# A two-block transformer: token order of five RWKV sources by full-array transpositions, and three small reductions in full-array records

## The reference

```python
def wkv_scan(s0, decay, k, v, kk, a, r, reverse):
    def step(S, inp):
        w_t, k_t, v_t, kk_t, kka_t = inp[:5]
        S = (S * w_t[:, :, None, :]
             - jnp.einsum('bhij,bhj->bhi', S, kk_t)[..., None] * kka_t[:, :, None, :]
             + v_t[..., None] * k_t[:, :, None, :])
        y = jnp.einsum('bhij,bhj->bhi', S, inp[5]) if emit else None
        return S, y
...
kk = kk * lax.rsqrt(jnp.maximum(jnp.sum(kk * kk, axis=-1, keepdims=True), 1e-24))
...
var = jnp.mean(jnp.square(y - mean), axis=-1, keepdims=True)
yn = ((y - mean) * lax.rsqrt(var + GN_EPS)).reshape(B, L, D_MODEL) * ln_g + ln_b
```

## Time and profile before

| | |
|---|---|
| median of the runs | 3081.94 us |
| the profiled execution, its own time | 3091.67 us |
| its span in the trace | 3089.9 us |
| mean granted TensorE clock | 0.947 |
| the eight rounds (start of the first to the end of the eighth) | 1252.5 to 1869.3 us |

### The profile page before, as it was taken

One profiled execution on the slowest core, in us unless ns is written; L12 is line 12 of the kernel. 1 busy time (PEld: TensorE's weight loads), 2 busy tenths in 40 slices (PEclk: granted clock), 3 DMA queues, 4 the chain that ended last, 5 costly groups with the idle time before them and its releaser, 6 DMA issues. The chain is left out here.

```text
span 3089.9 us, 72809 instructions
## 1 busy us (share of the span) xinstructions
PE 2705.3 (88%) x32492; PEld 2378.1 (77%) x32492; DVE 1848.7 (60%) x2902; ACT 1134.9 (37%) x1786; POOL 31.7 (1%) x46
## 2 busy tenths in 40 slices
PE   4988989999997998677777777899998898889998
PEld 4977989999996887566666676688886685678887
DVE  7656775655546643766666665755567644466642
ACT  4326343222224432533444333433334415454421
POOL 0011000000000000000000000000000000000000
PEclk9999989999996999799999998899998998999999
DMA  6320224444321333000000003355531210123332
GB/s 257 117 88 27 89 85 130 126 130 140 120 75 55 113 103 128 24 22 25 25 25 25 25 10 116 126 179 176 179 111 57 68 36 8 55 77 101 96 94 84
DMA packets 89958, 272.52 MB, mean 88 GB/s; under 512 B 9440, under 2 KB 14688, under 8 KB 89568
## 3 DMA queue, kind: packets, MB, share of 16 engines
q1 hardware_dynamic: 85088, 258.17, 25.5%
q10 hardware_dynamic: 4608, 10.49, 1.0%
HBM read 252.11 MB, written 16.52 MB: 87 GB/s over the span
## 5 line engine op out<-in xcount | busy, mean ns | idle before, releaser
L427 DVE TENSOR_TENSOR weights_low<-raw_weights,weights_high 128x1024 fp32r<-128x1024 f32 (+3 forms) x333 | 356.4, 1072 | 703.4 <-ACT weights_high L396 702.6
L396 ACT ACTIVATE weights_high<-raw_weights 128x1024 fp32r<-128x1024 f32 (+3 forms) x333 | 310.9, 935 | 970.9 <-PE psum L223 928.9
L223 PE MATMUL psum<-mlp_in_high,weights_high 128*128 128x512 f32 (+1 forms) x1120 | 370.3, 367 | 21.5 <-DVE mlp_in_low L964 16.4
L223 PE MATMUL psum<-mlp_in_low,weights_high 128*128 128x512 f32 (+1 forms) x1120 | 369.0, 366 | 0.0
L223 PE MATMUL psum<-mlp_in_high,weights_low 128*128 128x512 f32 (+1 forms) x1120 | 368.7, 366 | 0.0
L223 PEld LDWEIGHTS psum<-mlp_in_high,weights_high 128*128 128x128 f32 x1120 | 208.1, 189 | 49.3 <-issue 17.6
L223 PE MATMUL psum<-hidden_high,weights_high 128*128 128x384 f32 (+1 forms) x768 | 229.5, 352 | 0.0
L223 PE MATMUL psum<-hidden_low,weights_high 128*128 128x384 f32 (+1 forms) x768 | 229.5, 352 | 0.0
L223 PE MATMUL psum<-hidden_high,weights_low 128*128 128x384 f32 (+1 forms) x768 | 229.4, 352 | 0.0
L223 PEld LDWEIGHTS psum<-mlp_in_low,weights_high 128*128 128x128 f32 x1120 | 208.4, 189 | 23.9
L223 PEld LDWEIGHTS psum<-mlp_in_high,weights_low 128*128 128x128 f32 x1120 | 208.1, 189 | 24.0
(11 more groups left out here) (470 smaller groups left out, 5248.7 us busy)
## 6 DMA issues: line engine op xcount, KB each, us to landing
raw_weights<-in_mlp_w SPq DMA_DIRECT2D x96, 512.0 KB, 4.3
mod_space<-in_ada SPq DMA_DIRECT2D x56, 512.0 KB, 3.6
pool_u<-in_ada SPq DMA_DIRECT2D x56, 512.0 KB, 3.6
raw_weights<-in_w_up SPq DMA_DIRECT2D x44, 512.0 KB, 3.6
work<-in_ada SPq DMA_DIRECT2D x32, 512.0 KB, 4.9
raw_weights<-in_mlp_w SPq DMA_DIRECT2D x64, 256.0 KB, 3.1
raw_weights<-in_w_down SPq DMA_DIRECT2D x16, 512.0 KB, 3.5
raw_weights<-in_w_in SPq DMA_DIRECT2D x12, 512.0 KB, 4.7
```

The source lines that it names most:

```text
L223: last = nc.tensor.matmul(out[:, a, :] if wide else out, w[:, cols], x[:, at, t0:t1], start=first, stop=final)
L396: nc.scalar.activation(halves_of(ph, j)[0], raw_of(ph, j), ACT.Copy).then_inc(high.sem, 1)
L427: nc.vector.tensor_tensor(lo, raw_of(ph, j), hi.bitcast(F32), ALU.subtract).then_inc(split.sem, 1)
```

## The change

Five of the seven sources (V, both A, both KD) are turned by six 128 x 128 transpositions each; EXC stays at 24 small matmuls. V with A of direction 0, and A of direction 1 with KD of direction 0, share a batch of twelve over banks 4 to 6, with one count for TensorE and two keeps on ACT; so five batches take the place of seven, and each stands at another job of the list. `bonus` goes to bank 6, `step` and `ystate` to bank 7. `sums` and `yvar` are six and four matmuls of 128 x 128 weights on two columns. `root` and `groot` write their root widened over the head, 768 and 512 columns from a repeated input, and `spread` and `yspread` transpose that, six and four times; DVE's products with them are one instruction each. `bonus`, `sums`, `small` and `root` stand one job earlier. The waits of K, E, P and B for their turned sources name the same sources as before; E, which needs both EXC, now waits for the last batch of all. In the diff empty and unchanged lines are left out, and with them those four waits and the new bank numbers of `step`, `ystate`, `ysum` and of the bonus on DVE.

```diff
@@ -2077,10 +2077,10 @@
     at = {("M", 0): [("tok", 0), ("step", 1)], ("N", 0): [("tok", 1), ("step", 2)],
-          ("I", 0): [("tok", 2), ("step", 3)], ("M", 1): [("tok", 3), ("step", 4)],
-          ("N", 1): [("tok", 4), ("step", 5)], ("I", 1): [("square", 0), ("tok", 5), ("step", 6)],
-          ("M", 2): [("tok", 6), ("bonus", 0), ("step", 7)], ("N", 2): [("sums", 0), ("step", 8)],
-          ("I", 2): [("small", 0), ("root", 0), ("lora", 0), ("step", 9)], ("K", 0): [("lora", 1), ("step", 10)],
+          ("I", 0): [("step", 3)], ("M", 1): [("tok", 2), ("step", 4)],
+          ("N", 1): [("tok", 3), ("step", 5)], ("I", 1): [("square", 0), ("tok", 4), ("bonus", 0), ("step", 6)],
+          ("M", 2): [("sums", 0), ("step", 7)], ("N", 2): [("small", 0), ("root", 0), ("step", 8)],
+          ("I", 2): [("lora", 0), ("step", 9)], ("K", 0): [("lora", 1), ("step", 10)],
@@ -2193,7 +2193,9 @@
-    TURN, BONUS, PREPS = 6, 13, 14
+    TURN, BONUS, PREPS = 6, 11, 12
+    TURNS = ("V", "A0"), ("A1", "KD0"), ("KD1",), ("EXC0",), ("EXC1",)
+    TURNED = sum(TURNS, ())
@@ -2263,6 +2265,7 @@
+        ROOTS = sb("wkv_roots", [P, SEQ])
@@ -2569,31 +2572,43 @@
                     if name == "tok":
-                        src = (V[:, :], EXC[:, 0, :], EXC[:, 1, :], A[:, 0, :], A[:, 1, :], KD[:, 0, :], KD[:, 1, :])[n]
-                        if n == 0:
-                            pe.wait_ge(v_loaded.sem, v_loaded.base + 16 * (k + 1))
-                        if k or n >= 5:
-                            pe.wait_ge(tilded.sem, tilded.base + k + 1)
-                        elif n >= 1:
-                            pe.wait_ge(first_tilded.sem, first_tilded.base + 2)
-                        pe.wait_ge(*(turn_kept(k, n - 1) if n else prep_kept(k, 2)))
-                        if n == 0 and k >= 2:
-                            pe.wait_ge(pair_done.sem, pair_done.base + k - 1)
-                        for p in range(tiles):
...
-                            t = tile_of((n - 1) % 2, p) if 1 <= n <= 4 else p
-                            for o in range(2):
-                                for h in range(2):
-                                    f, to = rows_of(h), rows_of(p % 2 if 1 <= n <= 2 else o)
-                                    c = (p // 2 * 2 + o if 1 <= n <= 2 else p) * CHUNK
-                                    last = nc.tensor.matmul(ps[to, 4 + h, c:c + CHUNK], src[f, at_chunk(t, o)], EYE[f, :],
-                                                            start=True, stop=True)
+                        for m, what in enumerate(TURNS[n]):
+                            at = TURNED.index(what)
+                            source = {"V": V[:, :], "EXC0": EXC[:, 0, :], "EXC1": EXC[:, 1, :], "A0": A[:, 0, :], "A1": A[:, 1, :],
+                                      "KD0": KD[:, 0, :], "KD1": KD[:, 1, :]}[what]
+                            if what == "V":
+                                pe.wait_ge(v_loaded.sem, v_loaded.base + 16 * (k + 1))
+                                pe.wait_ge(*prep_kept(k, 2))
+                                if k:
+                                    pe.wait_ge(*by_vector(k - 1, "F", GROUPS - 1))
+                                if k >= 2:
+                                    pe.wait_ge(pair_done.sem, pair_done.base + k - 1)
+                            elif m == 0:
+                                pe.wait_ge(*turn_kept(k, at - 1))
+                            if k or what in ("KD0", "KD1"):
+                                pe.wait_ge(tilded.sem, tilded.base + k + 1)
+                            elif what != "V":
+                                pe.wait_ge(first_tilded.sem, first_tilded.base + 2)
+                            for p in range(tiles):
+                                if what in ("EXC0", "EXC1"):
+                                    t = tile_of(int(what[3]), p)
+                                    for o in range(2):
+                                        for h in range(2):
+                                            f, c = rows_of(h), (p // 2 * 2 + o) * CHUNK
+                                            last = nc.tensor.matmul(ps[rows_of(p % 2), 4 + h, c:c + CHUNK], source[f, at_chunk(t, o)],
+                                                                    EYE[f, :], start=True, stop=True)
+                                else:
...
+                                    t, to = (tile_of(int(what[1]), p), p % 2 * 3 + p // 2) if what in ("A0", "A1") else (p, p)
+                                    lo = 4 * 512 + m * T0 + to * P
+                                    last = nc.tensor.transpose(flat[:, lo:lo + P], source[:, t * P:(t + 1) * P], core.ident[:, :])
...
                     elif name == "bonus":
...
+                        pe.wait_ge(*turn_kept(k, TURNED.index("KD0")))
                         for h in range(2):
...
-                            last = nc.tensor.matmul(ps[f, 7, :], core.ones[f, 0:HEAD], BON[f, :], start=True, stop=True)
+                            last = nc.tensor.matmul(ps[f, 6, :], core.ones[f, 0:HEAD], BON[f, :], start=True, stop=True)
@@ -2611,11 +2626,8 @@
                         pe.wait_ge(squared.sem, squared.base + q + 1)
...
-                            for o in range(2):
-                                for h in range(2):
-                                    f = rows_of(h)
-                                    last = nc.tensor.matmul(ps[rows_of(o), 4 + h, t:t + 1], SQ[f, at_chunk(t, o)], core.ones[f, 0:1],
-                                                            start=True, stop=True)
+                            last = nc.tensor.matmul(ps[:, 4, 2 * t:2 * t + 2], SQ[:, t * P:(t + 1) * P], core.head_sum[:, 0:P:HEAD],
+                                                    start=True, stop=True)
@@ -2623,12 +2635,9 @@
                         pe.wait_ge(rooted.sem, rooted.base + q + 1)
...
-                            for h in range(2):
-                                for o in range(2):
-                                    f, c = rows_of(o), h * tiles + t
-                                    last = nc.tensor.matmul(ps[rows_of(h), 4 + o, t * CHUNK:(t + 1) * CHUNK],
-                                                            small[f, 0, 1, c:c + 1].to_broadcast([HEAD, HEAD]), EYE[f, :],
-                                                            start=True, stop=True)
+                            last = nc.tensor.transpose(flat[:, 4 * 512 + t * P:4 * 512 + (t + 1) * P],
+                                                       KK[:, t * P:(t + 1) * P],
+                                                       core.ident[:, :])
@@ -2670,21 +2679,15 @@
                     elif name == "yvar":
...
-                            for o in range(2):
-                                for h in range(2):
-                                    f = rows_of(h)
-                                    last = nc.tensor.matmul(ps[rows_of(o), 4 + h, tiles + t:tiles + t + 1], CSQ[f, at_chunk(t, o)],
-                                                            core.head_mean[f, h * HEAD:h * HEAD + 1], start=True, stop=True)
+                            last = nc.tensor.matmul(ps[:, 5, 2 * t:2 * t + 2], CSQ[:, t * P:(t + 1) * P], core.head_mean[:, 0:P:HEAD],
+                                                    start=True, stop=True)
...
                     elif name == "yspread":
...
-                            for h in range(2):
-                                for o in range(2):
-                                    f, c = rows_of(o), h * xt + t
-                                    last = nc.tensor.matmul(ps[rows_of(h), 4 + o, t * CHUNK:(t + 1) * CHUNK],
-                                                            small[f, 1, 1, c:c + 1].to_broadcast([HEAD, HEAD]), EYE[f, :],
-                                                            start=True, stop=True)
+                            last = nc.tensor.transpose(ps[:, 4, t * P:(t + 1) * P],
+                                                       ROOTS[:, t * P:(t + 1) * P],
+                                                       core.ident[:, :])
@@ -2727,21 +2730,19 @@
                     if name == "tok":
                         eng.wait_ge(prep_done.sem, prep_job(k, TURN + n))
-                        src = ps[:, 4:6, 0:tiles * CHUNK].rearrange("p h (t c) -> p h t c", c=CHUNK)
-                        if 1 <= n <= 2:
-                            d = n - 1
-                            dst = RHS[:, :, :, 2 * d:2 * d + 2, 0, :].rearrange("p i o h c -> p h (i o) c")
-                        elif 3 <= n <= 4:
-                            d = n - 3
-                            dst = AG[:, 2 * d:2 * d + 2, :, :, 0, :].rearrange("p j i h c -> p h i j c")
-                            for h in range(2):
-                                last = act(dst[:, h, :, :, :], src[:, h, :, :].rearrange("p (i j) c -> p i j c", j=2), ACT.Copy)
-                            last.then_inc(prep_s.sem, 1)
-                            return
```

(35 more changed lines are left out.)

18 lines of the change are left out of this document (9 added, 9 removed).

## The result

| | median us | runs | ratio to the kernel before, 95% |
|---|---|---|---|
| before | 3082.47 | 3079.83 to 3084.26 | |
| changed | 3055.71 | 3052.46 to 3061.24 | 0.9913 (0.99 to 0.9925) |
| changed, a second time, beside another set of runs of before (3083.09) | 3054.65 | 3049.45 to 3061.62 | 0.9908 (0.9892 to 0.9923) |

The change saves 27 to 28 us. The forecast was 3047, a saving of 35; the result lies inside the range and 8 to 9 us above the forecast. The profiled execution of the changed kernel took 3061.24 us, 30.4 less than that of before.

What follows compares the result with a forecast made beforehand. It took the first part of a round to be bound by TensorE's instruction fetch; 21.6 + 2.5 + 3.3 + 7.2 = 34.6 us, rounded to 35, taken from the median gave 3047 us, range 3020 to 3072.

Steps and rivals of the forecast that it cites:

- What bounds it: First part of a round: bound by the number of TensorE's instructions, fed at some 3.7 us for 256.
- By fetch alone 13.4 us: Up to the end of N of group 2: 454 records, 3.57 packets of 3.75 us, 13.4 for 19.2 us.
- rival (a): Fetch is all: every saved packet counts, 7.7 us a round, 60 in all, 3022 us; chance 0.15.
- By waits alone: First part with fetch free: ACT round trips set it; `sums` at 12.6 us, TensorE through N of group 2 at 14.4.
- the stall: First part: of 3.6 remaining fetch stalls of about 1 us, one, 1.0 us, lands on the chain.
- Switching shapes: 14 changes a round between four 64 x 64 arrays and one full array: 0.1 us each, 1.4 us a round.
- Rival (c): Each change of array shape drains TensorE, 0.45 us on the chain: 15 us slower, 3097 us; chance 0.05.
- The last part: Last part of a round: 52 records fewer, at most 1.6 us, against a longer `groot`; 0.9 us taken.
- the cover of `groot`: Last part: 1.1 us between the root's end and TensorE's `yspread`, gone if TensorE comes a whole microsecond earlier.
- The sum: Rounds 1 to 6 21.6 us, round 0 2.5, round 7 3.3, last part 7.2: 34.6 us saved, rounded to 35.
- (b): Round's first part: stalls hide behind waits for two keeps; gain 1.3 us a round, 10 in all, 3072 us; chance 0.18.
- (d): ACT's repeated input or keep across two banks runs at half speed, about 4 us a round lost, 3080 us; chance 0.07.

Runs made afterwards that it cites:

- e1_turn_only: Kernel before with V, both A and both KD turned by six 128x128 transpositions each, in seven single batches at the old places: 3061.19 us, ratio 0.9929.
- e11_two_turned: Kernel before with KD of both directions alone turned by six 128x128 transpositions: 3074.27 us, ratio 0.997.
- the four kernels above: Before (3082.47 us); before with two KD sources transposed (3074.27); before with five sources transposed in seven batches (3061.19); the changed kernel (3055.71).

## Why the prediction came out as it did

*What bounds it.* Right in kind: the "issue" gaps inside runs of like matmuls are TensorE without instructions; they fell from 28 to 2 in six rounds as records were taken out, and the half of the change that cuts the sources' records gives 22 of 28 us. What it expected to be left was too much: 3.6 stalls of about 1 us in the first part, where the first profile shows one stall up to N of group 2 in each of two rounds and none in four. The Trainium skill, "Runtime: NRT & Kernel Launch", Instruction fetch mechanics, calls such crossings "mostly hidden": up to N of group 2 they are so in the changed kernel, with 0.2 us a round of such stalls, and are not in the kernel before, with 3.7.

*"By fetch alone 13.4 us"* and rival (a), which rests on it, were impossible, and the trace of before said so: TensorE is busy for 15.0 us in that stretch, so no removal of instructions could end it sooner, and the text itself had found that TensorE's own time hardly changes. *"By waits alone"*, 14.4 us to the same place, fails by the same check: 15.0 us of work and 0.7 for `sums` do not fit into it. The check "652/127 = 5.13 packets, 3.75 us each" was circular: it divides the length by the count, and would have come out whatever bound the stretch. The right reading of the same row is 19.22 - 15.02 = 4.2 us of idle, the ceiling of the term; measured per round, 4.4 idle went to 1.3.

*"By waits alone"*, the term on which the sum stood. The steps of round 3 on TensorE:

```profile
1473.84 0.87 PE L2604 MATMUL psum<-constants,wkv_v 128*128 128x128 f32 x6
1474.55 0.82 PE L2604 MATMUL psum<-constants,wkv_a 128*128 128x128 f32 x6
...
1476.97 0.87 PE L2604 MATMUL psum<-constants,wkv_a 128*128 128x128 f32 x6 [0.76 <-ACT wkv_a_ga L2745]
...
1480.71 0.87 PE L2604 MATMUL psum<-constants,wkv_kd 128*128 128x128 f32 x6
...
1484.51 0.92 PE L2598 MATMUL psum<-wkv_eye,wkv_exc_rho 64*64 64x64 f32 x46 [0.21 <-ACT residual L2745]
...
1487.38 1.50 PE L2629 MATMUL psum<-constants,wkv_kk 128*128 128x2 f32 x12
...
1492.53 0.88 PE L2622 MATMUL psum<-lora_input,wkv_ups 64*64 64x384 f32 x8 [1.70 <-DVE wkv_small L2908]
```

and on ACT:

```profile
1475.40 0.81 ACT L2745 ACTIVATE work<-psum 128x768 f32<-128x768 f32 x1 [11.67 <-PE psum L2604]
1476.11 0.81 ACT L2745 ACTIVATE wkv_a_ga<-psum 128x768 f32<-128x768 f32 x1
...
1492.68 0.84 ACT L2762 ACTIVATE wkv_kk<-wkv_small 128x768 f32<-128x768 f32 x1 [6.33 <-DVE wkv_small L2910]
1493.54 1.28 ACT L2754 ACT_TABLE_LOAD   x1
1494.83 1.05 ACT L2754 ACTIVATE wkv_decay<-psum,wkv_parameters 128x384 f32<-128x384 f32 x2
```

| from the round's start, us | forecast | measured |
|---|---|---|
| second batch begins | 3.7 | 3.8 |
| `sums` begins | 12.6 | 14.2 |
| `sums` takes | 0.7 | 1.5 |
| TensorE through N of group 2 | 14.4 | 16.9 |
| `small` ends on DVE | 17.8 | 19.4 |
| ACT's first `lora` keep | 20.0, with the stall 21.0 | 21.6 |
| loop begins | 29.6 | 30.0 |

The batches, the keeps (0.81 us, also across the banks) and the root (0.84 us for the 0.81 taken) came as worked out. Two terms were too small. What comes on top of the batches (11.9 us) was given 0.7 us; it took 2.3, most of it since TensorE works in order: KD1's transpositions stand behind M of group 1 and come 0.7 us after their bank is free, EXC0 0.2 us late behind N of group 1, and `sums` behind the bonus and M of group 2, 1.0 us after ACT's last keep. And `sums` was priced as six transpositions, 0.66 us, although the prediction itself counts 12 records for it; it took 1.50. What made up for it: in this round no stall of fetch landed on the chain, where 1.0 us had been put, DVE's `small` came 2.5 us after TensorE where 3.4 had been allowed, and the chain from `lora` to the loop gave 0.5 us where 0.3 was forecast (8.88 to 8.34 us from ACT's first `lora` keep). So the first part lost 3.4 us in the mean of six rounds for the 3.6 forecast (3.5 in the second profile): a right total in which a stall that did not come paid for work that had been left out. That the total came out is luck.

*Switching shapes.* Right: 0.1 us each. The transpositions begin 0.06 us before the last 64 x 64 record of M ends (1473.21 + 0.69 against 1473.84), where like follows like at 0.17. Rival (c) is out by this and by the result; the drain of which "TensorEngine Tiling (Array Packing)" of the Trainium skill, Key Properties, speaks has this price here.

*The last part.* Forecast 0.9 us, measured 0.8 and 1.0. The terms are not those of the forecast: the cover of `groot` is gone, as it had warned (TensorE waits 0.36 us in round 3), and `yvar` takes 1.05 us in 8 records where 32 took 0.64; the shorter stalls pay for both.

*The sum.* Rounds 1 to 6 gave 4.2 and 4.5 us each in the two profiles, for 4.5. Round 0 gave 3.6 and 0.5 for 3.4, round 7 5.5 and 3.3 for 4.2. The sum for the rounds, 34.6, stands against 34 and 31. The medians show 27 to 28. The difference lies outside the rounds or in the profiled executions themselves: that of before was 9.7 us above its median, the two of the changed kernel 5.5 and 4.1; a round's saving read off a slow execution of before was taken in full from the median. Part of it can be placed: round 0 starts at 1252.5 us in that execution and between 1246.6 and 1249.2 in all eleven other profiles, at 1246.8 and 1246.6 in the two (`e1_turn_only`, `e11_two_turned`) whose code up to there is that of before. So some 6 of its 9.7 us lie ahead of the rounds, and no more than 4 can be in the 34 and 31 read off it. How the rest divides was not settled.

*The rivals.* (a) out, as shown. (b) lives in part: waits for ACT did come into the open, at 1 us a round and not the 3.5 that it takes back, and what took the place of fetch up to N of group 2 is above all TensorE's own work in order, busy for 94% of it. (d) is out: keep and root run at the speed forecast.

## What to carry to other kernels

Cutting the instructions of an engine that starves for them, while its work stays the same, gives back its idle time in that stretch and no more; read length less busy time first, and hold every forecast of the stretch, by fetch or by waits, against the busy time. Then ask which chain is late next: here starting `small`, `root` and the chain behind them one job earlier, with no work saved, gave 24 us, nearly as much as the whole change. And a fuller array isn't a cheaper record: price each shape by its own count of records.

## What the runs showed of the hardware that was not expected

- A matmul of 128 x 128 f32 weights on only two columns costs two transpositions. `sums` in the changed kernel, and the weight load of a transposition (`yspread`), each min/median/max ns:

```profile
L2629 PEld LDWEIGHTS psum<-constants,wkv_kk x12: 186/192/192, 1487.4 to 1488.6; 128*128 128x128 f32 x12
L2629 PE MATMUL psum<-constants,wkv_kk x12: 251/251/272, 1487.4 to 1488.6; 128*128 128x2 f32 x12
```

```profile
L2688 PEld LDWEIGHTS psum<-constants,wkv_roots x32: 137/142/231, 1390.6 to 1848.8; 128*128 128x128 f32 x32
```

  The weight load of a record is listed at 192 ns and that of a transposition at 142, but the records follow one another just as closely: (1.50 - 0.25)/11 = 0.11 us for `sums`, (0.87 - 0.27)/5 = 0.12 us for six transpositions of a source. The difference is the count: six matmuls leave twelve records, six transpositions six. The 48 small records that `sums` had before take 0.96 us, 0.02 each, so undoing it made the first part 0.4 us a round shorter with four times the records.
- Stalls on instructions vanish faster than the packets. The stretch up to N of group 2 is about 5.3, 4.6, 3.6 and 3.6 packets of 127 matmul records in the four kernels above, and the stalls are 3.7, 2.7, 0.6 and 0.2 us a round. TensorE's own work for a packet is 2.9, 3.3, 4.2 and 4.4 us (busy time by packets), and a packet took 3.50 to 3.70 us where it starved: stalls are few where the own work takes longer than that. The last two kernels differ in `sums`, the pairing and the places.
- An ACT instruction whose input repeats each element 64 times runs like a plain one: 0.84 us for 768 columns and 0.63 us for 512, where a plain keep of 768 from PSUM takes 0.81.
